# Values of the first attention branch projected for four heads at a time, the later branches' values put behind head 5, and a gate tile moved from ahead of the attention into its filling work

## The reference, cut to what matters

```python
def project_kv(p, lw, pos):
    ckv, kr, sk, sv, ak, av = _split(p, KV_SPLITS)
    kv_m = (rmsnorm(ckv, lw['mla_kv_norm']) @ lw['mla_w_ukv']).reshape(B, T, MLA_HEADS, MLA_NOPE + MLA_V)
    k_rope = rope(kr.reshape(B, T, 1, MLA_ROPE))
    k_m = jnp.concatenate([kv_m[..., :MLA_NOPE], jnp.broadcast_to(k_rope, ...)], axis=-1)
    v_m = kv_m[..., MLA_NOPE:]          # 8 heads x 64
    ...
    v_s = sv.reshape(B, T, SWA_KV_HEADS, SWA_HEAD_DIM)
    v_a = av.reshape(B, T, AX_KV_HEADS, AX_HEAD_DIM)

def hybrid_layer(x, ctx, c, c_ctx, lw, pos, update_ctx):
    ...
    o_m = dense_latent_attention(q_m, k_m, v_m, kc_m, vc_m, MLA_SCALE)
    o_s = window_latent_attention(q_s, k_s, v_s, kc_s, vc_s, sink, SWA_SCALE)
    o_a = dense_latent_attention(q_a, k_a, v_a, kc_a, vc_a, AX_SCALE)
    x = x + gate * merge_branches(o_m, o_s, o_a, z_m, z_s, z_a, g, lw)   # o * silu(z) @ w_o, gated by sigmoid(g), @ w_out
    if update_ctx:                       # layer 0 only: the same for the 256 context tokens
        ...
```

## Time and profile before

| what | value |
|---|---|
| timed runs | 1783.62, 1785.39, 1778.84 us, median 1783.62 |
| profiled execution | span 1785.1 us; the page gives it no other time of its own |
| PE busy | 1711.1 us, 96% |
| DVE, ACT, POOL busy | 1084.0, 1049.3, 528.0 us |
| DMA | 129.53 MB, 73 GB/s on average |
| mean granted TensorE clock | 0.980 of 2.4 GHz |
| mla attention of layer 0 | 168.6 to 361.4 us of the span |
| mla attention of layer 1 | 1136.4 to 1303.7 us |

### The profile page before, as it was taken

One profiled execution on the slowest core, in us unless ns is written; L12 is line 12 of the kernel. 1 busy time (PEld: TensorE's weight loads), 2 busy tenths in 40 slices (PEclk: granted clock), 3 DMA queues, 4 the chain that ended last, 5 costly groups with the idle time before them and its releaser, 6 DMA issues.

```text
span 1785.1 us, 27001 instructions
## 1 busy us (share of the span) xinstructions
PE 1711.1 (96%) x10554; PEld 1498.7 (84%) x10554; DVE 1084.0 (61%) x2185; ACT 1049.3 (59%) x1921; POOL 528.0 (30%) x300
## 2 busy tenths in 40 slices
PE   7999999999999999999999999999999999999997
PEld 3777888889989889899889996788888887888787
DVE  5543776765565566665775655477775756565634
ACT  3433778766666777666321253577776677786322
POOL 1523123222232212212322353322333432332442
PEclk9997999999999999999999999899999999999999
DMA  9111102111121111111644331111212221212642
GB/s 326 40 37 28 26 24 55 27 42 48 42 60 43 47 37 36 42 48 36 201 153 166 118 97 49 40 34 37 60 48 66 72 64 44 60 49 65 200 142 95
DMA packets 178527, 129.53 MB, mean 73 GB/s; under 512 B 21661, under 2 KB 167647, under 8 KB 178400
## 3 DMA queue, kind: packets, MB, share of 16 engines
q1 hardware_dynamic: 174242, 115.37, 22.7%
q10 hardware_dynamic: 2878, 8.24, 1.3%
q0 software_dynamic: 1280, 4.20, 0.7%
HBM read 123.58 MB, written 4.19 MB: 72 GB/s over the span
## 4 chain that ended last, share of the span: by engine, by line
PE 76%; DVE 10%; ACT 7%; issue 3%; POOL 2%; DMA 1%; SPq 0%; DVEq 0%; ACTq 0%; POOLq 0%
PE acc L1357 56%; PE wide L1415 6%; PE ptp L1435 6%; PE pv L1448 4%; PE pv L1449 3%; DVE nmax L1991 2%; ACT e L1682 2%; DVE pt L2016 1%; DMA w_raw<-in_ada_w 1%; POOL h_lo L1844 1%; DVE k_m L1552 1%; ACT w_hi L1600 1%; DVE k_s L1552 1%; DVE q_s L1552 1%; POOL w_lo L1806 1%
## 5 line engine op out<-in xcount | busy, mean ns | idle before, releaser
L1806 POOL TENSOR_TENSOR w_lo<-w_raw,w_hi 128x1024 fp32r<-128x1024 f32 (+2 forms) x192 | 392.0, 2045 | 1085.0 <-ACT w_hi L1600 1084.8
L1357 PE MATMUL acc<-h_hi,w_hi 128*128 128x512 f32 (+2 forms) x1320 | 463.3, 352 | 10.3 <-DVE cq_lo L1554 3.9
L1357 PE MATMUL acc<-h_hi,w_lo 128*128 128x512 f32 (+2 forms) x1320 | 462.0, 351 | 0.0
L1357 PE MATMUL acc<-h_lo,w_hi 128*128 128x512 f32 (+2 forms) x1320 | 457.7, 350 | 0.3 <-POOL h_lo L1844 0.3
L1991 DVE TENSOR_REDUCE nmax<-wide 128x1 f32<-128x768 f32 (+3 forms) x240 | 189.6, 790 | 167.9 <-PE wide L1415 166.2
L1357 PEld LDWEIGHTS acc<-h_hi,w_hi 128*128 128x128 f32 (+1 forms) x1320 | 248.4, 188 | 50.1 <-issue 7.9
L1697 ACT ACTIVATE pt<-ptp 128x512 fp32r<-128x512 f32 (+3 forms) x312 | 165.8, 563 | 210.4 <-PE ptp L1435 208.6
L1357 PEld LDWEIGHTS acc<-h_hi,w_lo 128*128 128x128 f32 (+1 forms) x1320 | 248.2, 188 | 33.4
L1357 PEld LDWEIGHTS acc<-h_lo,w_hi 128*128 128x128 f32 (+1 forms) x1320 | 246.1, 188 | 34.2 <-POOL h_lo L1844 0.5
L1689 ACT ACTIVATE e<-e,einv 128x768 f32<-128x768 f32 (+3 forms) x240 | 193.5, 806 | 70.2 <-DVE einv L2008 69.8
L2016 DVE TENSOR_TENSOR pt<-ptp,pt 128x512 fp32r<-128x512 f32 (+3 forms) x312 | 191.8, 640 | 43.9 <-ACT pt L1697 43.7
(11 more groups left out here) (216 smaller groups left out, 3103.1 us busy)
## 6 DMA issues: line engine op xcount, KB each, us to landing
w_raw<-in_w_in SPq DMA_DIRECT2D x102, 512.0 KB, 3.9
w_raw<-in_ada_w SPq DMA_DIRECT2D x48, 512.0 KB, 5.3
w_raw<-in_w_out SPq DMA_DIRECT2D x16, 512.0 KB, 4.2
w_raw<-in_w_in SPq DMA_DIRECT2D x16, 256.0 KB, 3.3
w_raw<-in_w_o_mla SPq DMA_DIRECT2D x16, 256.0 KB, 2.8
w_raw<-in_w_o_swa SPq DMA_DIRECT2D x16, 256.0 KB, 2.8
w_raw<-in_w_o_ax SPq DMA_DIRECT2D x16, 256.0 KB, 2.9
w_raw<-in_mla_w_uq SPq DMA_DIRECT2D x16, 144.0 KB, 2.4
```

Of the source, the lines that this page charges most:

```text
L1357: ins = nc.tensor.matmul(dst, lhs, rhs, start=first, stop=last)
L1806: nc.gpsimd.tensor_tensor(w_lo[s][:, 0:k], w_raw[s][:, 0:k], f(w_hi[s][:, 0:k]), ALU.subtract).then_inc(w_lo_ready, 1)
```

## The change

Values of mla are projected for four heads at a time: with head 0 for heads 0 to 3, with head 4 for heads 4 to 7, in three groups of two token tiles, each matmul with 256 moving columns. Each group is read out by two ACT and two DVE instructions (one for each pair of heads). `v_m` gets a third buffer, which lies over the first half of `v_s`; so `values_a`, which writes there, may now begin only when the output of head 5 has been issued, and it stands behind `values_b` in the queue. The chunks of weights are cut anew: the queries of heads 0 and 1 share one chunk, head 4's chunk holds keys and four heads' values, and the queries of head 5 get a chunk of their own. The gate tile `z` 1 is no longer projected ahead of the attention, but is the first `z` item of the queue.

```diff
@@ attention()
             if turned:
                 O(turned)
+                if turned["closes"]:
+                    issued["o", turned["branch"], turned["h"]] = n["s"]
@@ mla_head(h)
             if h % 2 == 0:
-                c = chunk("mk", l, h, h + 1 if h else 0)
+                four, heads = h % 4 == 0, (0, 1) if h == 0 else (h + 1,)
+                cq = chunk("mq", l, heads) if h == 0 else None
+                c = chunk("mk", l, h, None if four else h + 1)
...
-                vg = [group("vm", chunk_ids=(c,), mode="vm", l=l, cost=cost_of(128, 6 * 3), co=KKV * 2 * MLA_NOPE,
-                            tts=range(tt, tt + 3), what="vm", pair=h // 2, needs=lambda: latents) for tt in range(0, TT, 3)]
-                ready_v["mla", h // 2] = vg
-                qg = head_q(h + 1 if h else 0, c, KKV * 2 * (MLA_NOPE + MLA_V))
...
+                if four:
+                    vg = [group("vm", chunk_ids=(c,), mode="vm", l=l, cost=cost_of(256, 4 * 3), co=KKV * 2 * MLA_NOPE,
+                                tts=range(tt, tt + 2), what="vm", pair=h // 2, needs=lambda: latents) for tt in range(0, TT, 2)]
+                    ready_v["mla", h // 2] = ready_v["mla", h // 2 + 1] = vg
+                    cq = chunk("mq", l, heads) if cq is None else cq
+                    for i, hq in enumerate(heads):
+                        qg += head_q(hq, cq, i * KQ * MLA_K)
+                else:
+                    qg = head_q(h + 1, c, KKV * 2 * MLA_NOPE)
...
         usable[0] = TIGHT
         run_all(mla_head(0))
-        run_all(z_tile(l, 0, 1, zs, og))
-        flush()
@@ the queue
             if h % 2 == 0:
-                cost += cost_of(SEQ, 6) + cost_of(CTX, 6) + 2 * cost_of(128, 18)
+                cost += cost_of(SEQ, 6) + cost_of(CTX, 6)
+            if h % 4 == 0:
+                cost += 3 * cost_of(256, 12)
...
+        z_item(0, 1)
         z_item(0, 2)
-        item("values_a", "mla", cost_of(256, 72), lambda s: ("mla", 1 + len(tgs)) in s, values_s(0))
         z_item(0, 3)
         item("values_b", "mla", cost_of(256, 72), lambda s: ("mla", 5) in s, values_s(TT // 2))
+        item("values_a", "mla", cost_of(256, 72), lambda s: ("o", "mla", 5) in s, values_s(0))
@@ buffers
-    v_m = shared("v_m", [P, 2, TT, 2, 2, HD], R, 75776)
+    v_m = [shared(f"v_m{i}", [P, TT, 2, 2, HD], R, at) for i, at in enumerate((75776, 81920, 12288))]
@@ matmuls, mode "vm"
-                        c0 = g["co"] + k * 2 * MLA_V
-                        wv = [w[s][:, c0:c0 + 2 * MLA_V] for w in (w_hi, w_lo)]
+                        c0 = g["co"] + k * 4 * MLA_V
+                        wv = [w[s][:, c0:c0 + 4 * MLA_V] for w in (w_hi, w_lo)]
...
-                    run(a[:, i * 2 * HD:(i + 1) * 2 * HD], pairs)
+                    run(a[:, i * 4 * HD:(i + 1) * 4 * HD], pairs)
@@ reading out
+            if what == "vm":
...
+                for i in range(2):
+                    v = v_m[(g["pair"] + i) % 3][:, t0:t1]
+                    out_.append((v[:, :, :, 0, :], v[:, :, :, 1, :], got[:, :, 2 * i:2 * i + 2, :]))
+                return out_, None
```

More of the change, by code:

```diff
@@ L1115, in chunk_size @@
             if kind == "mk":
-                return KKV * 2 * (MLA_NOPE + MLA_V) + KQ * MLA_K
+                return KKV * 2 * MLA_NOPE + (KKV * 4 * MLA_V if chunks[c][3] is None else KQ * MLA_K)
             if kind == "mq":
-                return KQ * MLA_K
+                return len(chunks[c][2]) * KQ * MLA_K
             return KO * P if kind == "wo" else CHUNK
```

45 lines of the change are left out of this document (25 added, 20 removed).

## The result

The changed kernel takes 1799.18 us (median of 4 runs, 1795.96 to 1800.69), the kernel before 1783.38 beside it: a ratio of 1.0085, 95% interval 1.0062 to 1.0108. Forecast were 1779.2 us and a range of 1768 to 1793. The change makes the kernel slower, and the range didn't hold the time.

The account below looks back on a forecast made before the run. PE, busy 96% of the span, was taken as the bound, with the chain from scores to low probabilities beside it. Terms -15.1 + 1.0 - 1.8 + 8.5 + 3 gave -4.4 us, so 1779.2 us, range 1768 to 1793.

Parts of the forecast that it names:

- Matmuls removed: Values of mla: 288 matmuls of 128 columns become 144 of 256, saving 15.1 us; bounds -16.1 and 0.
- third rival: Merge buys nothing: a 256-column value matmul takes 0.22 us, only waits remain, +10.7, 1794.3 us; chance 0.03.
- Tile z 1 moved: Its 48 matmuls go from ahead of layer 0's attention into it: 0 in the matmul sum, brings cover.
- Reading out: Value read-outs on ACT and DVE, 24 narrower instructions each for 16: +1.0 us for both layers, bounds 0 and 4.2.
- Weights: Three more DMA and split instructions cost 0; PE's wait for a late POOL split in layer 1 goes: -1.8 us.
- Cover lost: Mla turns without filling work go from 1 to 6 in layer 0, 1 to 5 in layer 1: +8.5 us.
- The waits of `pv` for the low part: Layer 0 around heads 4 and 5: such waits in five places more, each 1.2 to 1.8 us.
- Idle time in the mla stages: Sign in the changed profile: PE idle some 16 us in layer 0 and 13 in layer 1.
- Clock: Two to four more falls to 1.2 GHz behind turns without filling work: +3 us, bounds 0 and 20.
- cold clock: Rival: four uncovered stretches each followed by 10.2 us at half clock, 5.1 lost each: 1796.6 us; chance 0.15.
- Sum: All terms over the whole span: -4.4 us, with the clock's +3 included.
- swa, ax and merge: Sign: these stages last what they do now; above 2 us difference would break the forecast in an unweighed place.

Follow-up runs that it names:

- e12: The kernel before, unchanged, run once more for a second profile; 3.4 us at half clock in its two mla stages, as in the first profile.
- e15: The changed kernel, run once more for a second profile; 41.0 us at half clock in its two mla stages, 37.5 in the first profile.
- e11: The kernel before with half of the value matmuls of heads 2 to 7 left out (12.1 us of filling work); 1789.5 us, ratio 1.0028.
- e3: The changed kernel with gate tile z 1 put back ahead of the attention; 1798.1 us.
- e2: The kernel before with values_a put behind values_b and waiting for head 5's output, no matmul saved; 1801.3 us.
- e8: The changed kernel with key, query and value groups interleaved and tile z 1 ahead of the attention; 1801.0 us.
- e10: The kernel before with values of heads 0 to 3 made together in two value buffers, head 2's groups interleaved, z 1 in the filling work; 1769.4 us.
- e9: The kernel before with tile z 1 in the filling work and head 0's weights cut as in the changed kernel; 1790.4 us.
- e4: The changed kernel with key, query and value groups of heads 2, 4 and 6 interleaved and head 4's first weight buffer kept longer; 1788.2 us.
- e14: The kernel with values of heads 0 to 3 together in two buffers (1769.4 us), with z 1 put back ahead of the attention; 1784.8 us.
- e5: The kernel before with late values_a, plus ten useless matmuls in each of twelve mla turns without filling work; 1800.1 us.
- e13: The changed kernel plus ten useless matmuls in each of eleven mla turns without filling work; 1794.9 us.
- e6: The changed kernel with interleaved groups, filling work held back until head 5's output so no turn is bare, z 3 waiting for head 3; 1810.0 us.

## Why the forecast was wrong

**Matmuls removed, -15.1.** The spacing was right: 0.12 us at 256 columns, 144 matmuls. Span less idle time less half of the time at half clock is 1674.7 us in the profile of before and 1658.3 in that after; in the second profiles, e12 and e15, it is 1675.5 and 1661.8. The differences, 16.4 and 13.7, lie about the 15.1. The step that failed stands in front of it: "a matmul that goes is time, as long as PE doesn't wait in its place". PE does wait in its place. The values of pair 0 cost the same ahead of the attention (36 x 0.112 there, 36 x 0.119 now); all that is saved was filling work in the attention, which I had called cover myself two sentences on. e11 gives 2 of 12 us in the rest; of 15.1 us e3 gives nothing against e2 (+2.2, good to 1.6), and e8, with the other order, 0.3, though part of their waits is for banks and weights. Where `values_a` stays early and only 7.6 us of matmuls go, e10 keeps 4.5 of them against e9. This one term is most of the error outside the clock. My third rival (the merge buys nothing) had the right size from a wrong cause.

The Trainium skill's section "LDWEIGHTS (loading the stationary operand)" of "TensorE: Matmul & The Clock Gate" was the better rule for the spacing: the trace has 0.12 us at 256 columns, above, and 0.11 at 128. The section "Wait — 56ns, not 53.3ns?" gives 0.109 and 0.056 for them. So the Trainium skill's objection to the merge fell on the price of a matmul, and in the rest the merge still gained nothing.

**Tile z 1 moved, 0.** Mis-sized. In a frame where its weights come in time the move gives -5.2 (changed kernel against e3), -6.8 (e4 against e8), -4.6 (e10 against e14) and -2.2 (e9 against before) in the rest. It was the good part of the change. In the clock its sign isn't settled: +6.2, -5.4, -9.0, +8.2.

**Reading out, +1.0, bounds 0 to 4.2.** Mis-sized: in the mla stages the waits for `k_m` and `v_m` are 10.5 us where they were 0.4. I had looked for bank waits in the first set of value groups alone. With heads 2 and 6 without value groups, key and query groups stand side by side, and head 4's value groups follow each other. e4 prices the order, with its kept buffer, at 4.1 us of rest and 11.0 us in time.

**Weights, -1.8.** Right: the wait of 1.8 us is gone.

**Cover lost, +8.5.** For the late `values_a` alone e2 has +7.1, so the size was about right. The working behind it was not. The waits of `pv` for the low part, forecast in five places more in layer 0, are one place and 1.7 us more there, and with those for `o_half` the chain's waits in both stages are 5.3 us more (profile of before and changed). Idle time in the mla stages was forecast at 16 and 13 us and is 16.8 and 20.0. Layer 0's figure is met by luck: 5.1 of its 6.1 us more (the kernel before had none of them there) are waits for `k_m` and `v_m`, which belong to the point above; in layer 1 these are 5.4. The sum for a wide turn also leaves out ACT's exponential, 0.99 us in the earlier trace rows, which stands between the scores and the low part; one such wait, at 270 us, took 2.4 us where 1.7 was taken.

**Clock, +3, bounds 0 and 20.** It is +11.0, mis-sized: about 18 more in the two mla stages, near my upper bound, less some 10 elsewhere, of which I had nothing. I expected falls of 3.4 us behind units 32 to 35; there are seven of 3.4 to 10.2 us in the two stages, the first while head 4's values are made. The rival "cold clock" is the nearest to what happened, with its 1796.6; it had 10.2 us falls in four places and none of the lost savings, so its nearness is luck. (The fall at 1313 us, which I put behind the thin end of layer 1's mla, lies 18.5 us behind that end.)

**Sum.** By the experiments in the rest: values late +7.1, merge with its order +2.2 (e3 less e2, good to 1.6), tile -5.2, together the measured +4.1 where I had -7.4; clock +11.0 where I had +3. This chain of differences closes by construction; that each link is real is shown by the others of its kind (e8, e4, e14). That swa, ax and merge last what they do now did not hold in layer 0. From the first row maximum of swa to the layer's last addition it takes 672.4 and 674.3 us in the two profiles of before, 676.7 and 678.9 in those of the changed kernel, over 4 us more for the same matmuls:

```profile
366.80:1039.20 672.40, 667.12 (x4365) 606.94 (x4364) 418.69 (x868) 380.98 (x742) 172.77 (x93) 0.99 0.25 73
...
369.80:1046.50 676.70, 669.57 (x4365) 607.90 (x4364) 419.12 (x868) 381.07 (x742) 173.89 (x93) 0.99 0.25 73
```

PE idles 7.1 us in it instead of 5.3. By the prediction's own mark, 2 us, this is a place that it hadn't weighed. In layer 1 the same stretch is 2.4 us shorter in the first pair and 1.5 in the second.

**Left open.** What sets the clock loss beyond idle time. e9 has 1.6 us less idle than before and 8 us more clock loss; e10 has as much idle as e9 within 2 us and 14 us less clock loss, part of it the shorter falls over head 0's values. Falls within the mla stages come with late values alone (e2, 27.3 us at half clock for 3.4) and with filling work left out alone (e11, 17.1 us). That idle in bare turns brings them is likely from e5's layer 0, but e5's layer 1 and e13's profile don't bear it out. How much of the waiting in e4, e6 and e8 is for weights kept back by the other order is open, too, and so is what lengthens layer 0 behind mla.

## What to carry to other kernels

Before booking removed work as saved time, ask whether it was the work that another engine's chain was hidden behind; leaving out such work altogether and changing nothing else (e11) is the quickest test, and here it made the kernel slower. When a group goes from an order that alternates banks, look at which two groups become neighbours. And split every run's time by its granted clock: the part that the clock doesn't explain repeats to one to three microseconds here, so it shows effects that the medians hide. When a forecast of idle time comes true, look at what the idle time waits for before you call it right.

## What the hardware showed that I had not expected

Useless matmuls in idle time need not cost anything: with 12.3 us of them the clock loss was 6.4 us lower and the median 4.3, though the profile doesn't show the gain where they stand (e13). Making the values of head 0 for four heads at once went with shorter falls ahead of the attention, 3.4 us or none for 6.8 to 13.7. Inside the span the clock falls come in lengths of 3.4, 6.8 and 10.2 us (one of 13.7 in e9), and their sum in one and the same kernel is anything from 50 to 86 us (twice the clock loss), which is nearly the whole scatter between its runs. A fall can come behind 14.4 us in which PE was busy 11.8 (82%) at 2.4 GHz, as in the windows above, while the earlier trace rows has one stretch of 12 us with 9.5 busy (79%) and no fall behind it.
